# A two-block transformer kernel: the hand-over from the odd layer's output product to the recurrent layer, rewritten in pieces of 512 columns

## The reference

```python
# end of the first block
x = x + y_odd @ od_w_out            # the odd layer's output product, 18 x 128 deep
x = rms_norm(x, final_norm_g)       # x * rsqrt(mean(x*x) + EPS) * g, row by row
# start of the second block, recurrent layer
h_lat = rms_norm_2(x,   norm_g[0]) * (1 + scale)  + shift
h_ctx = rms_norm_2(ctx, norm_g[0]) * (1 + cscale) + cshift
u_lat, g_lat = split(h_lat @ lru_w_in)       # 2048 -> 2 x 2048
u_ctx, g_ctx = split(h_ctx @ lru_w_in)
# then per block of 128 columns: a convolution over four tokens, two pairs of gates
# (128 x 128 products), two linear scans over the tokens, a product with silu(g)
```

## Time and profile before

| what | value |
|---|---|
| median of three runs | 2668.7 us |
| profiled execution, its time | 2669.98 us |
| its span | 2667.9 us |
| TensorE (PE) matmuls busy | 2527.2 us, 95% |
| VectorE (DVE) busy | 1430.2 us, 54% |
| ScalarE (ACT) busy | 1162.6 us, 44% |
| GpSimd (POOL) busy | 215.5 us, 8% |
| chain that ended last, by engine | PE 89%, DVE 3%, ACT 3%, DMA 2%, issue 1% |
| granted TensorE clock, mean | 0.976 of full speed |

### The profile page before, as it was taken

How to read it: one execution, slowest core, us unless ns; L and a number is a source line. 1 busy time by engine, 2 the same in 40 slices (tenths; PEclk the granted TensorE clock), 3 DMA queues, 4 the chain that set the end, 5 groups by cost and what they waited for, 6 DMA issues and landing times.

```text
span 2667.9 us, 31379 instructions
## 1 busy us (share of the span) xinstructions
PE 2527.2 (95%) x11984; PEld 1972.5 (74%) x11984; DVE 1430.2 (54%) x1900; ACT 1162.6 (44%) x1698; POOL 215.5 (8%) x120
## 2 busy tenths in 40 slices
PE   6999999979999999997999999999799999999988
PEld 5887777747876666686777777788587777777767
DVE  4644545524545454465376676633546374653664
ACT  6544434513454434355456556422424334253442
POOL 0000000000000000001355554000000000000000
PEclk9999999988999999998999999999899999999999
DMA  6556677655577888864233332323234243242323
GB/s 219 182 182 214 224 246 245 215 191 203 182 239 261 288 279 276 285 236 132 79 94 90 94 94 92 110 79 101 81 97 133 80 126 94 87 133 79 118 88 126
DMA packets 275111, 425.07 MB, mean 159 GB/s; under 512 B 14374, under 2 KB 92988, under 8 KB 273852
## 3 DMA queue, kind: packets, MB, share of 16 engines
q1 hardware_dynamic: 273596, 418.09, 48.0%
q10 hardware_dynamic: 1408, 5.51, 0.5%
HBM read 421.45 MB, written 2.10 MB: 159 GB/s over the span
## 4 chain that ended last, share of the span: by engine, by line
PE 89%; DVE 3%; ACT 3%; DMA 2%; issue 1%; SPq 0%; ACTq 0%; DVEq 0%
PE ps L694 63%; PE ps L1038 13%; PE ps L766 3%; PE ps L1045 2%; PE ps L842 1%; ACT ring_hi L1249 1%; PE ps L1130 1%; DMA ring<-in_ev_w_out 1%; PE ps L1148 1%; PE ps L869 1%; DMA ring<-in_od_w_in 1%; PE ps L777 1%; PE ps L742 1%; DVE ring_lo L1671 1%; PE ps L854 1%
## 5 line engine op out<-in xcount | busy, mean ns | idle before, releaser
L1249 ACT CAST ring_hi<-ring 128x1024 fp32r<-128x1024 f32 (+2 forms) x590 | 611.5, 1039 | 1150.2 <-PE ps L694 742.9
L1671 DVE TENSOR_TENSOR ring_lo<-ring,ring_hi 128x1024 fp32r<-128x1024 f32 (+2 forms) x526 | 632.8, 1210 | 798.3 <-ACT ring_hi L1249 795.2
L694 PE MATMUL ps<-ring_hi,act_hi 128*128 128x512 f32 (+2 forms) x1272 | 511.8, 402 | 16.4 <-DVE ring_lo L1671 9.2
L694 PE MATMUL ps<-ring_hi,features_hi 128*128 128x512 f32 x1152 | 463.3, 402 | 35.3 <-DVE features_lo L2080 14.2
L694 PE MATMUL ps<-ring_hi,act_lo 128*128 128x512 f32 (+2 forms) x1272 | 493.6, 388 | 0.0
L694 PE MATMUL ps<-ring_lo,act_hi 128*128 128x512 f32 (+2 forms) x1272 | 492.8, 387 | 0.0
L694 PE MATMUL ps<-ring_hi,features_lo 128*128 128x512 f32 x1152 | 454.2, 394 | 0.0
L694 PE MATMUL ps<-ring_lo,features_hi 128*128 128x512 f32 x1152 | 454.2, 394 | 0.0
L694 PEld LDWEIGHTS ps<-ring_hi,act_hi 128*128 128x128 f32 x1272 | 241.2, 190 | 106.9 <-issue 31.0
L694 PEld LDWEIGHTS ps<-ring_hi,features_hi 128*128 128x128 f32 x1152 | 219.4, 190 | 104.2 <-issue 41.4
L694 PEld LDWEIGHTS ps<-ring_hi,act_lo 128*128 128x128 f32 x1272 | 240.8, 189 | 50.7
(11 more groups left out here) (229 smaller groups left out, 2308.0 us busy)
## 6 DMA issues: line engine op xcount, KB each, us to landing
ring<-in_mod_w SPq DMA_DIRECT2D x192, 512.0 KB, 5.4
ring<-in_att_w_in SPq DMA_DIRECT2D x128, 512.0 KB, 3.6
ring<-in_ev_w_in SPq DMA_DIRECT2D x104, 512.0 KB, 4.5
ring<-in_od_w_in SPq DMA_DIRECT2D x96, 512.0 KB, 5.4
ring<-in_lru_w_in SPq DMA_DIRECT2D x64, 512.0 KB, 4.0
ring<-in_ev_w_out SPq DMA_DIRECT2D x40, 512.0 KB, 3.6
ring<-in_od_w_out SPq DMA_DIRECT2D x36, 512.0 KB, 3.6
ring<-in_lru_w_out SPq DMA_DIRECT2D x32, 512.0 KB, 3.5
```

The source lines that it names most:

```text
L694: mm = pe.matmul(PS[:, bank, 0:n], a, w[:, k - k0, :], start=(k == k_first and j == 0), stop=(k == k_last and j == 2))
L1249: act.copy(high(U, n), raw(U, n)).then_inc(s_hi, 1)
L1671: dve.tensor_tensor(out=low(U, n), in0=raw(U, n), in1=high(U, n).bitcast(F32), op=ALU.subtract).then_inc(s_lo, 1)
```

## The change

1. **X is multiplied by FG before its statistics are known**, chunk by chunk, into XG (the memory of XN): chunks 0 to 2 by GpSimd, chunk 3 by VectorE. ScalarE sums the squares of X (SQX) and of XG (SQG) per chunk. With a = 1/(mean(x²)+EPS) and q = a/(a·mean(xg²)+EPS), the square root of (a, q) is taken in one instruction; XG times the root of q is the doubly normalised row.
2. **Normalised rows come per chunk and per half of the rows**: VectorE makes rows 0 to 127, ScalarE rows 128 to 255, and TensorE transposes a chunk when both are there.
3. **Context features are made inside chunk 3 of the odd output product**: j = 4, 5, 6, 7 and 2 behind units 28, 30, 32 and 34; j = 0, 1 and 3 behind unit 35.
4. **The first block of the recurrent layer is multiplied in two token halves**, 256 columns a matmul: first the 256 context columns, with transposes of x between, then the x columns, each k as soon as its features are there.
5. **The rescaling of X itself** (old line 2024) moves behind the first `conv`; it now raises `s_y`.
6. Gates and products of the loop become functions; the first block stands before the loop, whose first pass is written out.

```diff
+CTX_BEHIND = {28: (4,), 30: (5,), 32: (6,), 34: (7, 2), 35: (0, 1, 3)}
@@ TensorE
-            for u in range(9, 36):
-                od_out(u)
-            pe.wait_ge(s_re, RES0["lru_out"])
...
-            to_features(tiles_of(CN))
-            pe.wait_ge(s_xn, 2)
-            to_features(tiles_of(XN))
+            for u in range(9, 27):
+                od_out(u)
...
             pe.wait_ge(s_xn, 1)
+            assert fills[0] == FEATURES_CTX
+            for u in range(27, 36):
+                od_out(u)
+                for j in CTX_BEHIND.get(u, ()):
+                    to_features(tiles_of(CN), j, 1)
+            def lru_first(part, half, lat):
+                U = UNIT0["lru_in"] + part * 2 + half
+                split_ready(U)
+                if not lat:
+                    pe.wait_ge(s_xl, FEATURES_CTX + (4 if half else 8))
+                    if part == 0:
+                        pe.wait_ge(s_re, RES0["od_out"] + 3)
+                    else:
+                        pe.wait_ge(s_re, RES0["od_out"] + 4)
+                tokens = slice(lat * SEQ, (lat + 1) * SEQ)
+                for k in range(8):
+                    kk = half * 8 + k
+                    if lat:
+                        pe.wait_ge(s_xl, FEATURES_CTX + 8 + kk // 2 + 1)
+                    for j, (W, x) in enumerate(((high(U), FTH), (high(U), FTL), (low(U), FTH))):
+                        mm = pe.matmul(PS[:, part * 2, tokens], W[:, k * P:(k + 1) * P], x[:, kk, tokens],
+                                       start=(kk == (0 if lat else 8) and j == 0), stop=(kk == (KT - 1 if lat else 7) and j == 2))
+                if lat:
+                    mm.then_inc(s_wused, 1)
+            def lru_normal(c):
+                pe.wait_ge(s_xn0, c + 1)
+                pe.wait_ge(s_xn1, c + 1)
+                to_features(tiles_of(XN), 2 * c, 2)
+            lru_first(0, 1, 0)
+            lru_first(1, 1, 0)
+            lru_first(0, 0, 0)
+            lru_normal(0)
+            lru_first(1, 0, 0)
+            lru_normal(1)
+            lru_normal(2)
+            lru_first(0, 0, 1)
+            lru_normal(3)
+            lru_first(0, 1, 1)
+            lru_first(1, 0, 1)
+            lru_first(1, 1, 1)
...
+            lru_gates(0)
+            lru_products(1)
+            lru_gates(1)
+            with pe.Fori(1, KT // 2) as i:
@@ ScalarE
-            for c, end in enumerate((22, 31, 36)):
-                hi_to(O + end)
...
-            root(5, 2)
...
-            root(6, 2)
...
+            hi_to(O + 22)
+            x_squares(0)
+            xg_squares(0)
+            hi_to(O + 31)
+            x_squares(1)
+            xg_squares(1)
...
+            for u in range(27, 36):
+                follow([("od_out", u)])
+                for j in CTX_BEHIND.get(u, ()):
+                    scale_features(mod_scale(1), mod_shift(0, 1), TMP_B, j, 1)
+                if u == 28:
+                    x_squares(2)
+                if u == 30:
+                    xg_squares(2)
+            x_squares(3)
+            xg_squares(3)
+            act.wait_ge(s_ms, 6)
+            act.activation(ST[:, 5, 0:4], ST[:, 5, 0:4], ACT.Sqrt).then_inc(s_rt, 2)
+            act.wait_ge(s_rt, 6)
+
+            def rows1_normalized(c):
+                cols = slice(c * CHUNK, (c + 1) * CHUNK)
+                act.activation(XN[:, 1, cols], XG[:, 1, cols], ACT.Copy, scale=ST[:, 5, 3:4]).then_inc(s_xn1, 1)
+            rows1_normalized(0)
+            rows1_normalized(1)
+            scale_features(mod_scale(0), mod_shift(0, 0), TMP_B, 0, 2)
+            rows1_normalized(2)
+            scale_features(mod_scale(0), mod_shift(0, 0), TMP_B, 2, 2)
+            rows1_normalized(3)
+            scale_features(mod_scale(0), mod_shift(0, 0), TMP_B, 4, 4)
@@ VectorE
+            for u in range(27, 36):
+                lo_to(min(O + u + HIS, O + 36))
+                for j in CTX_BEHIND.get(u, ()) if u < 35 else ():
+                    split_features(part(FTH, 0), part(FTL, 0), TMP_B, j, 1)
             residual_add("od_out", 3)
...
+            for tt in range(TT):
+                ins = dve.tensor_tensor(out=XG[:, tt, last], in0=X[:, tt, last], in1=FG[:, last], op=ALU.mult)
+            ins.then_inc(s_xg, 1)
+            for j in CTX_BEHIND[35]:
+                split_features(part(FTH, 0), part(FTL, 0), TMP_B, j, 1)
...
+            dve.wait_ge(s_sqc, 8 * TT)
+            dve.tensor_reduce(of_g, SQG, AX, ALU.add)
+            link(dve.tensor_reduce(a, SQX, AX, ALU.add))
+            link(dve.tensor_scalar(a, a, 1.0 / D, EPS, ALU.mult, ALU.add))
+            link(dve.reciprocal(a, a))
+            link(dve.tensor_tensor(out=of_g, in0=of_g, in1=a, op=ALU.mult))
+            link(dve.tensor_scalar(of_g, of_g, 1.0 / D, EPS, ALU.mult, ALU.add))
+            link(dve.reciprocal(of_g, of_g))
+            dve.tensor_tensor(out=q, in0=of_g, in1=a, op=ALU.mult).then_inc(s_ms, 2)
+            dve.wait_ge(s_rt, 6)
+            dve.sem_inc(s_rs, 2)
+
+            def rows0_normalized(c):
+                cols = slice(c * CHUNK, (c + 1) * CHUNK)
+                dve.tensor_scalar(XN[:, 0, cols], XG[:, 0, cols], ST[:, 5, 2:3], None, ALU.mult).then_inc(s_xn0, 1)
+            rows0_normalized(0)
+            rows0_normalized(1)
+            split_features(part(FTH, 1), part(FTL, 1), TMP_B, 0, 2)
+            rows0_normalized(2)
+            split_features(part(FTH, 1), part(FTL, 1), TMP_B, 2, 2)
+            rows0_normalized(3)
+            split_features(part(FTH, 1), part(FTL, 1), TMP_B, 4, 4)
...
             conv(block_n(0), 0)
+            for tt in range(TT):
+                ins = dve.scalar_tensor_tensor(out=X[:, tt, :], in0=X[:, tt, :], scalar=ST[:, 5, tt:tt + 1], in1=FG, op0=ALU.mult, op1=ALU.mult)
+            ins.then_inc(s_y, 2)
@@ GpSimd
+            for c in range(3):
+                cols = slice(c * CHUNK, (c + 1) * CHUNK)
+                pool.wait_ge(s_re, RES0["od_out"] + c + 1)
+                for tt in range(TT):
+                    ins = pool.tensor_tensor(out=XG[:, tt, cols], in0=X[:, tt, cols], in1=FG[:, cols], op=ALU.mult)
+                ins.then_inc(s_xg, 1)
```

More of the change, by code:

```diff
@@ L494, in build @@
         NLAM = SC[:, 436:437]
-        SQX, SQL, SQC = (SC[:, j:j + 8].rearrange("p (t c) -> p t c", t=TT) for j in (72, 56, 64))
+        SQX, SQL, SQC, SQG = (SC[:, j:j + 8].rearrange("p (t c) -> p t c", t=TT) for j in (72, 56, 64, 80))
+        XG, JUNK_C = XN, BUF[:, 16384:16384 + CHUNK]
         MSC = SC[:, 440:504]
@@ L1011, in _ @@
                     sum_mod(N_MOD - 1)
-            for u in range(9, 36):
+            for u in range(9, 27):
                 od_out(u)
-            pe.wait_ge(s_re, RES0["lru_out"])
             pe.wait_ge(s_xn, 1)
-            to_features(tiles_of(CN))
-            pe.wait_ge(s_xn, 2)
-            to_features(tiles_of(XN))
-            with pe.Fori(0, KT // 2) as i:
-                for b in range(2):
[L1024 to L1047, removed]
@@ new lines, in _, with lru_gates @@
+            lru_first(1, 1, 1)
+            def lru_gates(b, i=None):
+                n = lambda plus: at(b + plus, i, 2)
+                pe.wait_ge(s_xc, n(3))
+                pe.wait_ge(s_gw[b], at(64, i, 64))
+                pe.wait_ge(s_sg, n(1))
+                for j in range(4):
+                    mm = pe.matmul(PS[:, 4 + j, :], GW[:, b, j, :], XC[:, b, :, :].rearrange("p c s -> p (c s)"),
+                                   start=True, stop=True)
+                mm.then_inc(s_gt, 1)
@@ new lines, in lru_products @@
+            def lru_products(b, i=None):
+                n = lambda plus: at(b + plus, i, 2)
+                pe.wait_ge(s_xc, n(1))
+                for part in range(2):
+                    if part:
+                        pe.wait_ge(s_gs, n(1))
+                    for half in range(2):
+                        U = UNIT0["lru_in"] + b * 4 + part * 2 + half
+                        split_ready(U, i, 8)
+                        for k in range(8):
+                            w = slice(k * P, (k + 1) * P)
+                            kk = half * 8 + k
+                            for j, (W, x) in enumerate(((high(U), FTH), (high(U), FTL), (low(U), FTH))):
+                                mm = pe.matmul(PS[:, part * 2 + b, :], W[:, w], x[:, kk, :],
+                                               start=(kk == 0 and j == 0), stop=(kk == KT - 1 and j == 2))
+                        mm.then_inc(s_wused, 1)
@@ L1457, in _ @@
             act.wait_ge(s_ctx, 16)
-            squares(4, token_tiles(CX), BUF[:, 0:D])
+            squares(4, token_tiles(CX), BUF[:, 14336:16384])
             hi_to(O + 18)
@@ L1461, in _, with x_squares, xg_squares @@
             act.wait_ge(s_sq, SQUARED[4])
-            for c, end in enumerate((22, 31, 36)):
-                hi_to(O + end)
+            def x_squares(c):
                 act.wait_ge(s_re, RES0["od_out"] + c + 1)
[L1465 to L1470, removed]
-            root(5, 2)
```

(19 more changed lines are left out.)

33 lines of the change are left out of this document (12 added, 21 removed).

## The result

| | before | after |
|---|---|---|
| median, us | 2667.93 (2665.61 to 2672.61, 4 runs) | 2648.1 (2644.61 to 2650.39, 4 runs) |
| ratio, 95% interval | | 0.9923 [0.9908, 0.9939] |
| profiled execution: time, span | 2669.98, 2667.9 | 2644.61, 2642.3 |
| granted TensorE clock, mean | 0.976 | 0.983 |

The changed kernel is 19.8 us faster in the median. Run again later beside the kernel before (5 runs against 11) it had 2648.07 against 2670.22, ratio 0.9912 [0.9898, 0.9927], 22.2 us. The forecast was 2645.3, in a range of 2641 to 2654.

What follows compares the result with a forecast made beforehand. TensorE was taken to carry the end, with 56.1 us from product to first gates. Gates at 1242.2 + 30.1 = 1272.3 instead of 1295.71 gain 23.4 us, taken off the median of 2668.7: 2645.3, range 2641 to 2654.

Steps and rivals of the forecast that it cites:

- Context features inside the product: Five sets of transposes before the product's end, some 0.53 us each; their ScalarE and VectorE work costed at nothing.
- T: End of od_out(35), the last unit of the odd output product; forecast to move from 1239.6 to 1242.2 us.
- From T to the first transposes of x: Product's end to first x transposes: chunk 3 added by T+3.2, scale at T+10.1, first rows at T+10.8 as context halves end.
- the eight small instructions: VectorE's small instructions after the three splits, before the root: between 1.3 and 4.2 us, taken as 1.9.
- From these transposes to the gates: Chunk 0 transposed to T+11.9, last half ended at T+29.9, gates at T+30.1; VectorE and ScalarE set the pace T+17 to T+23.5.
- The sum: First gates at 1272.3 instead of 1295.71 us, 23.4 us gained, bounds 17 to 26; given 0.79.
- D: Measured distance from the start of unit 30's high part in the odd output product to the first gate matmul; 80.5 us before.
- The rescaling behind conv: X's rescaling, 4.62 us, leaves the critical way; done at T+32 if nothing holds it, needed at T+33.5; lateness costed at nothing.
- the lock's rival: GpSimd's low parts make the rescaling 3 to 6 us late past the gates; 2 to 5 us given back; chance 0.08.
- The clock: Rival: small waits in the hand-over drop TensorE's clock, costing 10 us, gain 13, 2655; chance 0.05.
- The loop didn't tip over: Slower rival: block 0's lateness makes TensorE wait 2.1 us at each of 14 gates, 30 us lost, 2675; chance 0.05.
- The high parts weren't starved: Hardly-any-change rival: added sets and squares starve high parts from unit 27, some 2 us at nine units, gain 5 or less; 0.03.

Runs made afterwards that it cites:

- earlier context sets: Changed kernel with context sets one or two units earlier, behind 28, 29, 30, 32, 33, 34 and two behind 35; ratio 0.9906, again 0.9912, to the kernel before.
- the kernels with added lateness: Changed kernel with 16 or 32 linked VectorE instructions behind the rescaling, sigmoids 8.6 or 16.0 us later; first to last gates 387.5 and 394.9 us against 381.2.
- late context sets: Changed kernel with all eight context sets behind unit 35 of the product; ratio 0.9958 to the kernel before.
- old statistics: Changed kernel with two roots, X rescaled, squared and normalized whole as before, early context sets and halves kept; ratio 0.9944 to the kernel before.

## Why the prediction was right, and where it was off

The forecast, faster by 17 to 26 us, came true with 19.8 and 22.2. Point by point:

*Context features inside the product* cost nothing but their transposes, as forecast. From the high part of unit 30 to T it is 26.6 us instead of 24.4, 2.2 more; I had 2.65, and a set took 0.44 us instead of 0.53.

*From T to the first transposes of x* is the step that failed in size, by 2.4 us. With T at 1238.54, the context splits behind unit 34 were to end at T+1.9 and did at T+4.3; chunk 3 was to be added by T+3.2; it was at T+5.5. GpSimd's low parts held these splits up twice, for 1.4 and 2.1 us (1.81 against 0.42, 2.80 against 0.69), more than I had let them, and every later step shifted. The first rows came at about T+12.6 instead of T+10.8, though the eight small instructions took 1.5 us, against 1.9 taken. TensorE didn't wait for these rows: its context halves ended only then, delayed by the 2.8 us of waits for the addition and for the last splits (1.32 and 1.45), and the transposes started at T+13.2 (1251.70) instead of T+10.8. The kernel with earlier context sets takes these waits away, by moving the same splits ahead, and gives 2.3 us back: its gates start at T+29.8, where the forecast had T+30.1.

*From these transposes to the gates*: 19.4 us (T+13.2 to T+32.6), forecast 19.3. VectorE and ScalarE set the pace of the last x features as described. Only the grouping of transposes was different: three groups, since chunks 1 and 2 follow on each other.

*The sum*: gates at T+32.6, not T+30.1, T itself 0.4 less late: D fell by 21.3 instead of 23.4.

*The rescaling behind conv* met GpSimd twice, as the lock's rival had it, but the first time for only 0.3 us: its two halves took 2.66 and 4.44 us instead of 2.31 each, 7.02 in all, done at 1275.30, 0.45 behind the gates' end. ScalarE's sigmoids started at 1276.26, behind a load of their table that runs meanwhile, so nothing was lost. Moving it was worth 2.0 us, not 4.6.

*The rivals.* The lock never reached the end: the kernels with added lateness show a cushion of 5.3 us at the second gates, of which the change uses almost nothing. The clock stayed at 1.00 in the hand-over of the changed kernel, in both its traces. In four kinds of kernel (no halves, late context sets, old statistics, late sigmoids) it fell behind a pause of TensorE of 3.3 us or more. With the halves alone it fell to 0.50 at 1241.2 behind waits of 1.46 us and less, while the changed kernel kept it through 1.32 and 1.45. So short waits can be enough; what decides isn't shown, and this rival was nearer than the 0.05 I gave to it. The prediction's sentence that only the long pause of the trace of before shows a fall holds for the hand-over alone: from 560 to 620 us that trace has 0.82, 0.75 and 0.66 in stretches of 20 us. The loop didn't tip over even 16 us late. The high parts weren't starved.

What the parts are worth depends on each other: taken out of the change singly, the halves cost 15.7, the statistics with the moved rescaling 6.0 and the early context sets 3.9 by D (8 to 11 by the medians), together 25.6 by D for a gain of 21.3. The moved rescaling by itself is worth 2.0, which is no fourth part, as the 6.0 hold it already. Taken alone, the halves bring 10.5.

## What to carry to other kernels

A pause of TensorE between two layers is filled by splitting the next product along whatever is ready early; that needs the early part's inputs to be made under the layer before, and neither brings its full worth without the other. Where VectorE and GpSimd work at the same time on operands in on-chip memory, plan them as one engine: count every GpSimd instruction that falls into the critical stretch in full. VectorE instructions whose input was in PSUM weren't held up: the first of `conv` took 0.81 us beside a low part (1265.20) and 0.80 without one (1288.15). And measure such a change by a distance between two TensorE events around it, not by the time alone: here it repeated within 0.1 us in three kernels, where the times of one kernel scattered by 7 to 14. Take the times as well: with late context sets D promised 6 us more than the medians gave.

## What the runs showed that I had not expected

The time scatters before the change's place: unit 30 began anywhere from 1209.3 to 1222.2 us in the traces, though the kernels hardly differ up to there. The stretch from 540 to 660 us, in which no two kernels differ, had a granted clock of 0.82 to 0.89 from trace to trace; in the first 120 us it was 0.94 to 0.99, from there to 540 and from 660 to 1200 us 0.99 or 1.00.

The clock fell behind short pauses: behind 3.58 us of waiting it was 0.56 in the next 3 us (late context sets), around the end of 4.53 it was 0.51 over 6 us (old statistics), and with the halves alone it fell behind waits of no more than 1.46 us, while the changed kernel, with 1.32 and 1.45 us of waiting 3 us apart, kept 1.00. Gates that had been waited for took 5.4 to 6.0 us instead of 3.43.
